# Norms cut into parts, a reordered branch merge and an earlier fourth expert half in a two-layer float32 trunk

## What is computed

```
for i in range(DEPTH):                       # 2 layers
    xn = rms_norm(h, norm_mix[i])
    proj = xn @ w_in[i]                      # branches A, B, C and the gates pg
    ya = stick_breaking_attention(...)
    yb = ((groupnorm(rwkv recurrence) * ln_g + ln_b) + bonus) * g
    yc = swa_sink_attention(...)
    ga, gb, gc = split(sigmoid(pg))
    merged = ga*(ya @ w_proj_a) + gb*(yb @ w_proj_b) + gc*(yc @ w_proj_c)
    h = h + merged @ w_out[i]
    hn = rms_norm(h, norm_ffn[i])
    h = h + (swiglu(hn) if i == 0 else top-2-of-8 experts(hn))
return rms_norm(h, norm_final)[:, 16:]
```

## Time and profile before

| | us |
|---|---|
| median of 3 runs | 2392.31 (2390.92 to 2393.53) |
| the profiled execution | 2395.66 |
| its span, first to last instruction | 2392.7 |

### The profile page before, as it was taken

The page is one execution under the profiler, slowest core; times in us unless marked ns, Lnnn a source line. Parts: engine busy times, 40 slices in busy tenths (PEclk is TensorE's granted clock), DMA queues, the critical chain, the costliest instruction groups (busy, mean ns, idle before and its releaser), DMA issues.

```text
span 2392.7 us, 35192 instructions
## 1 busy us (share of the span) xinstructions
PE 2181.8 (91%) x14894; PEld 1850.8 (77%) x14894; DVE 1398.5 (58%) x1206; ACT 1196.7 (50%) x1116; POOL 22.3 (1%) x24
## 2 busy tenths in 40 slices
PE   7998985969999899998597799999999999999996
PEld 4757685969999675768597688888888787888885
DVE  2512336454444342133544688888888888888884
ACT  2134244323333123524432577777777777777673
POOL 0000010000000000001000000000000000000000
PEclk9998998979999899999898799999999999999998
DMA  5222101424444122110142498989898898989891
GB/s 184 111 66 108 71 3 71 177 82 184 168 176 161 71 106 88 71 71 3 53 171 95 168 370 316 371 321 364 336 357 351 338 367 314 373 317 376 322 371 76
DMA packets 73545, 484.38 MB, mean 202 GB/s; under 512 B 12392, under 2 KB 13544, under 8 KB 15704
## 3 DMA queue, kind: packets, MB, share of 16 engines
q1 hardware_dynamic: 69672, 478.62, 51.8%
q10 hardware_dynamic: 3760, 4.09, 0.6%
HBM read 480.94 MB, written 1.74 MB: 202 GB/s over the span
## 4 chain that ended last, share of the span: by engine, by line
PE 85%; DVE 8%; ACT 3%; issue 2%; DMA 1%; DVEq 0%; ACTq 0%; SPq 0%
PE PS L440 19%; PE PS L442 18%; PE PS L441 18%; PE PS L521 5%; PE PS L758 5%; PE PS L686 3%; DVE area L1456 3%; PE PS L493 2%; PE PS L633 2%; DVE WL L1456 2%; PE PS L607 2%; PE PS L647 1%; PE PS L482 1%; PE PS L965 1%; PE PS L1024 1%
## 5 line engine op out<-in xcount | busy, mean ns | idle before, releaser
L1456 DVE TENSOR_TENSOR WL<-ring,WH 128x2048 fp32r<-128x2048 f32 x414 | 944.1, 2290 | 333.5 <-ACT WH L1093 195.6
L1389 ACT ACTIVATE WH<-ring 128x2048 fp32r<-128x2048 f32 x336 | 643.3, 1916 | 189.5 <-PE PS L442 144.9
L440 PE MATMUL PS<-WH,XGH 128*128 128x512 f32 x896 | 356.1, 397 | 14.3 <-DVE WL L1456 11.0
L442 PE MATMUL PS<-WL,XGH 128*128 128x512 f32 x896 | 349.8, 390 | 0.0
L441 PE MATMUL PS<-WH,XGL 128*128 128x512 f32 x896 | 349.3, 390 | 0.0
L1093 ACT ACTIVATE WH<-ring 128x2048 fp32r<-128x2048 f32 x78 | 148.9, 1910 | 164.3 <-PE PS L442 164.3
L440 PEld LDWEIGHTS PS<-WH,XGH 128*128 128x128 f32 x896 | 168.3, 188 | 52.6 <-DVE WL L1456 15.9
L442 PE MATMUL PS<-XL,WH 128*128 128x272 f32 x704 | 204.2, 290 | 0.0
L442 PEld LDWEIGHTS PS<-WL,XGH 128*128 128x128 f32 x896 | 168.2, 188 | 36.0
L441 PEld LDWEIGHTS PS<-WH,XGL 128*128 128x128 f32 x896 | 168.4, 188 | 33.3
L440 PE MATMUL PS<-WH,HTH 128*128 128x512 f32 x448 | 176.7, 394 | 0.7 <-DVE WL L1456 0.2
(11 more groups left out here) (290 smaller groups left out, 3217.5 us busy)
## 6 DMA issues: line engine op xcount, KB each, us to landing
ring<-in_experts SPq DMA_DIRECT2D x336, 1024.0 KB, 6.9
ring<-in_weights SPq DMA_DIRECT2D x114, 1024.0 KB, 6.8
ring<-in_weights SPq DMA_DIRECT2D x4, 576.0 KB, 6.1
ring<-in_weights SPq DMA_DIRECT2D x4, 512.0 KB, 4.0
cst<-in_consts ACTq DMA_DIRECT2D x1, 1316.0 KB, 7.5
area<-in_x ACTq DMA_DIRECT2D x2, 512.0 KB, 4.4
out<-area SPq DMA_DIRECT2D x2, 512.0 KB, 2.6
bias_line<-lin SPq DMA_DIRECT2D x1, 672.0 KB
```

Source lines behind the costliest of these rows:

```text
L440: pe.matmul(o, lh, rh, start=first, stop=False, skip_group_check=True)
L442: return pe.matmul(o, lh, rl, start=False, stop=last, skip_group_check=True)
L1389: act.activation(WH[(BASE + j) % 3][:, :], ring[b][:, 2048 * (j % 2):2048 * (j % 2) + 2048], ACT.Copy).then_inc(S("w_hi"), 1)
L1456: tt = lambda o, a_, b_, op: dve.tensor_tensor(o, a_, b_, op)
```

## The change

- **Norms.** `hT`'s update, the squares and their sums go in three parts, tiles 0 to 3, 4 to 5 and 6 to 7 (`PARTS`). DVE's `added` adds a part and signals `h_sum`, ACT's `square` works on a part, PE's `norm` adds a part. For the norm before the feed-forward part the first part's sum stands between the two halves of O1. Matmuls signal in the middle of a half (`o_mid`, `f_mid`, `f_late`). The barriers around the norms of the layers go. What follows a norm waits for four scaled tiles at a time (`xn_done`).
- **Group norm and merge.** The barrier between them goes. P0 runs as soon as its operands and the eviction of the variances are there. The order of the branches is 0, 2, 1. The reciprocal is cut in four (`spread`) and stands, with the rest of the group norm (`scaled`, `normed`), between DVE's subtractions. A product with the gate is written over the gate itself, so the next gate waits for `m_free`.
- **Loads.** Layer 1's low-rank weights are issued on ACT's queue before layer 0's recurrence (four DMAs) and no longer in its merge.
- **Dense part.** Its first weight half is rounded and subtracted during O1.
- **Experts.** Four halves (`AHEAD`) of the next expert are made before the loop's jump and the update of `hT`; the selections move to behind halves 10 and 22.
- **End.** The output goes out in four DMAs of 256 KB and not in two of 512 KB.

```diff
+MERGE_ORDER = (0, 2, 1)
...
-        for b in range(3):
+        for b in MERGE_ORDER:
...
+        AHEAD = 4
...
-            def norm(l, which):
-                pe.wait_ge(S("sq_done"), at("sq_done", l, which) if l < DEPTH else 2 * DEPTH + 1)
-                for k in range(KT):
-                    ins = pe.matmul(PS[:, 0, 0:T], C("ones"), SQ[:, k, :], start=(k == 0), stop=(k == KT - 1))
-                ins.then_inc(S("sum_done"), 1)
+            def norm(l, which, parts=(0, 1, 2)):
+                for i in parts:
+                    pe.wait_ge(S("sq_done"), part(l, which, i))
+                    for k in range(*PARTS[i]):
+                        ins = pe.matmul(PS[:, 0, 0:T], C("ones"), squares_of(l, which)[:, k, :], start=(k == 0), stop=(k == KT - 1))
+                if 2 in parts:
+                    ins.then_inc(S("sum_done"), 1)
...
-                end_stage(pe, "pe")
...
+                            if j == 0 and half == 0 and d_ == 4:
+                                pe.wait_ge(S("n_e"), at("n_e", l, 0))
...
+                        if (h, half) == (1, 0):
+                            norm(l, 1, (0,))
-                end_stage(pe, "pe")
-                norm(l, 1)
-                end_stage(pe, "pe")
+                norm(l, 1, (1, 2))
...
+            def square(l, which, i):
+                lo, hi = PARTS[i]
+                act.wait_ge(S("h_sum"), part(l, which, i))
+                act.activation(squares_of(l, which)[:, lo:hi, :], hT[:, lo:hi, :], ACT.Square).then_inc(S("sq_done"), 1)
...
+                if l == 0:
+                    low_rank(1, lambda d_, s_: act.dma_start(d_, s_).then_inc(S("low_rank1"), 16))
...
+                act.activation(YH[0][:, :, :], yA[:, :, :], ACT.Copy).then_inc(S("x_hi"), 1)
+                high_half(first_split[l])
                 act.wait_ge(S("n_d"), at("n_d", l, 0))
-                act.activation(K[:, :, PADC:TP], Y[:, :, PADC:TP], ACT.Square).then_inc(S("n_sq"), 1)
-
-                high_half(first_split[l])
+                act.activation(GN[:, :, :], Y[:, :, PADC:TP], ACT.Square).then_inc(S("n_sq"), 1)
+                high_half(first_split[l] + 1)
                 act.wait_ge(S("n_e"), at("n_e", l, 0))
-                act.activation(K[:, :, PADC:TP], K[:, :, PADC:TP], ACT.Sqrt).then_inc(S("n_s"), 1)
-                high_half(first_split[l] + 1)
-                end_stage(act, "act")
-
-                act.activation(YH[0][:, :, :], yA[:, :, :], ACT.Copy).then_inc(S("x_hi"), 1)
+                act.activation(GN[:, :, :], GN[:, :, :], ACT.Sqrt).then_inc(S("n_s"), 1)
...
+            def added(i, sem, count):
+                q = slice(*PARTS[i])
+                dve.wait_ge(S(sem), count)
+                tt(hT[:, q, :], hT[:, q, :], PS[:, q, 0:T], ALU.add).then_inc(S("h_sum"), 1)
...
-                    dst = TMP[:, :, :] if b else MG[:, q, :]
-                    tt(dst, SG[:, q, :], PS[:, q, 0:T], ALU.mult).then_inc(S("m_read"), 1)
+                        tt(SG[:, q, :], SG[:, q, :], PS[:, q, 0:T], ALU.mult).then_inc(S("m_read"), 1)
+                        dve.wait_ge(S("m_read"), at("m_read", l, 2 * j + h))
+                        if j == 2:
+                            dve.wait_ge(S("m_free"), at("m_free", l, h))
+                        tt(MG[:, q, :], MG[:, q, :], SG[:, q, :], ALU.add).then_inc(S("m_free"), 1)
...
+                after_half(events, l, f"G{first_gate}0", 0).append((branch_low, 1))
+                after_half(events, l, f"G{first_gate}0", 0).append((spread, 1))
+                after_half(events, l, f"G{first_gate}0", 1).append((spread, 2))
+                after_half(events, l, f"G{first_gate}0", 1).append((spread, 3))
+                after_half(events, l, f"G{first_gate}1", 0).append((scaled,))
+                after_half(events, l, f"G{first_gate}1", 1).append((normed,))
...
+                at_half(events, "g", 2, 0, 0).append((select_rows, 2))
+                at_half(events, "g", 4, 0, 0).append((select_tokens, 4))
                 for j in range(3, HALVES):
-                    expert_low(n, j)
+                    if j >= AHEAD:
+                        expert_low(n, j)
```

More of the change, by code:

```diff
@@ L458, in columns_half, with rows_half @@
                         ins = three_products(PS[:, bank0 + dt, 0:T], wh[:, c], wl[:, c], xh(k), xl(k), k == 0, k == KT - 1)
+                    if mid and dt == 1:
+                        ins.then_inc(S(mid), 1)
                 ins.then_inc(S("w_used"), 1)
-            def rows_half(l, name, half, xh, xl, first, last, before=None, mid=None):
+            def rows_half(l, name, half, xh, xl, first, last, before=None, mid=None, late=None):
                 g = split_half[(l, name)] + half
@@ L1118, in _ @@
             for l in range(DEPTH):
-                norm(l, 0)
-                end_stage(act, "act")
+                if l == 0:
+                    for i in range(3):
+                        square(0, 0, i)
+                root(l, 0)
                 def projected(t):
@@ L1459, in _ @@
             v(dve.memset(egc[:, :, :], 0.0))
-            end_stage(dve, "dve")
             def low_half(g):
@@ L1873, in first_select @@
                 gathered_low(run * (NE + 1) + 1)
+                for j in range(3, AHEAD):
+                    expert_low(run * NE, j)
             for_all_experts(dve, expert_hidden, first_select)
             end_stage(dve, "dve")
-            norm(DEPTH, 0, "norm_final").then_inc(S("fin"), 1)
+            for i in range(3):
+                dve.memset(small[:, 50 + i:51 + i], 0.0).then_inc(S("h_sum"), 1)
+            norm(DEPTH, 0, "norm_final")
     return nc
```

282 lines of the change are left out of this document (166 added, 116 removed).

## The result

| | before | after |
|---|---|---|
| median (lowest to highest) | 2392.66 (2390.92 to 2393.53), 4 runs | 2311.56 (2308.94 to 2317.06), 4 runs |
| ratio | | 0.9665, 95% interval 0.9644 to 0.9686 |
| profiled execution; span | 2395.66; 2392.7 | 2317.06; 2315.3 |

A forecast was written before the change was run, and what follows sets the result against it. PE, busy 91% of the span, was taken as the bound, with gains only in its waits, mainly around norms. Savings of 33.4, 10.8, 8.7, 7.9, 2.8, 2.4, 10.5, less 1.0, made 75.5: 2392.3 to 2317 us, range 2302 to 2333.

The forecast's parts named there:

- Group norm: Between head means and G20: P0 starts once YL is ready, G20 waits 1.5 us; 16.7 us saved per layer, 33.4 in all.
- Inner norms: Norm before layer 0's dense part and layer 1's first and second norms: shorter gaps save 10.8, 8.7 and 7.9 us.
- Last norm: At the kernel's end: sums start after a shorter first square, PE goes on after four scalings; 2.4 us saved.
- Low-rank loads: Four DMA issues on ACT before layer 0's recurrence cost 1.0 us, bounds 0 and 2.2; their old place was idle.
- First norm: At the start: sums begin after a square of about 1.1 us, PE goes on after four scalings; 2.8 us saved.
- Experts: At changes of expert: four halves ahead remove PE's waits for WL; 10.5 us saved, ends 0 and 11.2.
- experts bound by the loads: Rival, chance 0.10: in the experts, waits for WL become waits for the ring, the 10.5 us is lost; 2327.5.
- a wait for the DMA in the experts: Sign in the profile after: if PE waited for the DMA in the experts, the prediction would be wrong.
- the 2319: Sum if the fixed latency per instruction charges two more squares in each of five norms, 0.2 us each on the path.
- the likeliest case: Whole kernel: the summed forecast, 2317 us, spanning 2311 to 2323 through experts', low-rank and handoff bounds; chance 0.57.
- the first rival: Chance 0.15: the clock falls before G20, costing 2 x 2.8 us, and more if norms' restarts are slower; 2325.
- the clock stays up: Rival, chance 0.10: shorter gaps keep the clock high at dense part, layer 1's first products and P0; 2309 us.

The follow-up runs named there:

- r3: Changed kernel with the first quarter of the group norm's reciprocal moved behind DVE's first gated products, in both layers; 2305.65 us, ratio 0.9642 to the kernel before.
- r12: Changed kernel with layer 1's low-rank weight loads issued back behind the merge, without the wait on their landing; 2312.07 us.
- r1: The changed kernel run again unaltered, timed against the kernel before; 2310.93 us, ratio 0.9662.
- r4: Changed kernel with all eight matmuls of the norm's sums behind O1, none between its halves, in both layers; 2309.44 us.
- r6: Changed kernel with the group norm's part undone: whole norm on DVE ahead of the first WL, barrier ahead of P0; 2339.46 us, ratio 0.9784.
- r7: Changed kernel with barriers back around the three inner RMS norms, their work still in parts; 2320.31 us.
- r10: Changed kernel with only the selections back at the head of each expert's DVE work, four halves ahead kept; 2310.68 us.
- r5: Changed kernel with the experts' part undone: three halves ahead, both selections at the head of the expert's DVE work; 2327.79 us, ratio 0.9726.
- r11: Kernel before with the experts' part of the change alone, four halves ahead and selections moved; 2374.03 us, ratio 0.9932.
- r8: Changed kernel with late start-up loads, the later quarter reciprocal, all sums behind O1, and P0's YL made ahead of DVE's first WL; 2307.19 us.

## Why the prediction was right, and where it was not

**Group norm: right.** 33.0 us measured between the first two profiles for 33.4. The mechanism is as worked out: P0 can start when YL is there (377.2 forecast, 377.09), and DVE is late for the first gate (wait of 1.5 forecast, 1.70 and 1.42; G20 at 392.4 forecast, 392.33). That the starts agree to a tenth is luck: the head means came 0.5 us earlier than before (367.04), and the variances took 2.74 us for 2.10. r3 took the wait away by moving the quarter reciprocal. The other quarters and the scalings are hidden, as forecast.

**Inner norms: right.** 11.8, 9.3 and 8.1 for 10.8, 8.7 and 7.9. **Last norm:** 3.5 for 2.4. **Low-rank loads:** 1.2 for 1.0, with r12 as its proof. "The place they left was idle" held for the kernel before, but not after the change.

**First norm: the step failed in its assumption, not in its chain.** "PE begins its sums after a first square of about 1.1" takes the square's own start as given. From ACT's table load to the first product the chain takes 30.51 - 11.26 = 19.25 us before and 34.11 - 17.72 = 16.39 after: 2.9 less for the 2.8 forecast. What sets its start is ACT's queue: the issue of the last start-up loads took 4.3 us in the profile before, 10.0 in the first profile after and 5.3 in r1. In the seven profiles with the new norm and the old place of these loads in which ACT's table load begins between 11.0 and 12.8, the first product stands between 27.4 and 28.9 (r1, r3, r4, r6, r7, r10, r12); in the two with it at 16.7 (r5) and 17.7 (the first), it stands at 31.8 and 34.1. Before it stood at 30.5, and at 32.0 in r11. So the gain is there in most executions, and 3.6 was lost in the one profiled.

**Experts: a mis-sized term.** I took 10.5 with 11.2 as the upper end, from the waits for WL that PE's own row shows. The part is worth 14.7 in the stretch alone (r11), 17.1 and 16.9 at the medians (r11, r5). The upper bound was to be read from the row of the weight load, 16.5: r11's 14.7 lies between the two rows, and so does r5's 18.8 against r1 (13.1 and 22.1). The first pair shows 9.1, with 3.5 taken back by the late load and the fall of the clock behind it. Rival "experts bound by the loads" is wrong as a limit: r11 and r1 ran the stretch in 1000.7 and 1002.3 us, with DMA share 0.88. But the loads are near enough to matter: the waits of PE for WL that are left with four halves ahead (one in the first profile, four in r12) each stand behind a load that came late. The prediction had a wait for the DMA in the experts as a sign of being wrong, and to that extent it was there.

**Clock: neither rival as told.** It was down at P0 in both kernels, as the sum had it (mean 0.51 from 373 to 380 us after). The new waits of 1.4 to 1.7 us before G20 left it up, as forecast, and r8's of 3.2 and 3.6 brought it down, so the rival named the right place but not this kernel. The one fall that nobody had forecast stands behind the experts' wait of 1.81 us. Elsewhere the clock was up more often than before, which I had costed at zero; in layer 0's attention r11 shows the same with the old code, so that part is no gain of the change. The Trainium skill (TensorE: Matmul & The Clock Gate, HAM oscillation) describes bursts that start cold behind long waits. r8 fits it; r4's 3.39 us in layer 1, which left the clock up, and the 1.81 us of the experts, which did not, show that here the length of the wait alone doesn't decide.

**Cutting the squares.** The rule of the Trainium skill on a fixed latency per instruction (VectorE: DVE Perf Modes, the TRN2 errata) is visible in ACT's rows: squares of 1088, 544 and 544 columns take 1.12, 0.66 and 0.66 us, 2.44 together, where one took 2.02: 0.2 a piece. But only the last square is on the path, and the 2319 that the rule would give is further off than 2317.

**The sum.** At the medians the change gave 81.1 us for 75.5. The experts, short by 4 to 6.6 us, are about that difference; the three inner norms and the last one gave 2.9 more than forecast. In the profiled execution, 2317.06, the start came 6.4 us worse than forecast and the experts 1.4, against 7.4 us in stages that the forecast left alone and a profile before that lay 3.3 above its median. The agreement to 0.1 us is chance; the forecast is to be compared with 2311.56.

Some of the forecast's figures don't follow from its terms. With the bounds named for the likeliest case (experts 11.2, low-rank 0) the lower end is 2315, not 2311; with the clock up and all of the 3.3 us it is 2303, not 2302; and the first rival adds 2 where it says "as much again" of 5.6. So the measured median lies below the likeliest case as its terms have it, and the mis-sized experts are the main reason. It lies near the 2309 of the rival "the clock stays up", but not for that rival's reason: behind all three places that it names, P0, the dense part's and layer 1's first product, the clock was down for 2 us or more after the change too (0.50 from 377 to 379, 507 to 509 and 775 to 779 us).

The runs undo the group norm's part, the barriers, the experts' part and the place of the low-rank loads. The order of the branches, the dense part's first half ahead, the parts of the norms and the four output DMAs were not tried alone; what is said of them rests on the stretches of the profiles.

## What to carry to other kernels

Size a stall on operands from the weight load's wait as well as from PE's: in both comparisons here (r11 with before, r5 with r1) the gain lay between the two. When a chain leaves the critical path, list the waiting engine's next operations in order and ask which of them the first consumer needs; moving one operation of 1.85 us, then one of 2.3, was worth more than further shortening of the chain. Issues of DMAs stand in the issuing engine's stream: put those that nobody needs soon behind the first work of that engine.

## What was unexpected of the hardware

- The issue of the same two DMAs (192 KB) held ACT for 1.0 us in a quiet moment, for 4.0 to 5.3 us in nine starts and for 9.4 and 10.0 us in two, while the weights' and constants' loads were under way.
- The same wait of 3.39 us ahead of layer 1's O0 was followed by the lower clock in one execution and not in the other, with the same instructions ahead of it (r1 and r4). In the experts a wait of 1.81 us was followed by it (the first profile after), the eight of 1.0 to 1.7 us in r5 and the seven in the profile before were not.
- Short waits of the weight load lengthen a run of matmuls without a gap in PE's row: in r11 3.4 us of PE's busy time went with the waits, the clock being 1.00 in the stretch in both kernels.
